# Activation buffers moved by 64 bytes within their partition, in a two-block transformer kernel in float32 precision

## The reference, cut to what matters

```
# first block, per layer
h = rms_norm(x, g) * (1 + sc1) + sh1
x = x + g1 * hybrid_mixer(h)               # w_in, two linear-attention halves, w_out
h = rms_norm(x, g) * (1 + sc2) + sh2
x = x + g2 * ((silu(h @ w1) * (h @ w3)) @ w2)       # layer 0, hidden width 2816
x = x + g2 * sum_e gate_e * swiglu(h, w1[e], w3[e], w2[e])   # layer 1, 8 experts, top 2
# second block, per layer: ffn, mixer (short convolution, then latent attention), ffn
h_x = h_x + 0.5 * m[2] * swiglu(pre(h_x)) ; h_c the same for the context
```

## Time and profile before

| | |
|---|---|
| device time, median of 3 runs | 2835.23 us (2834.12 to 2836.9) |
| the profiled execution | 2839.29 us |
| its span, first to last instruction | 2837.6 us |
| mean granted clock of TensorE | 0.989 |
| busy TensorE | 2720.8 us (96%) |
| busy VectorE, ScalarE | 1913.8 us (67%), 1182.6 us (42%) |
| matmuls | 17542, each with its LDWEIGHTS |

### The profile page before, as it was taken

How to read it: one execution, slowest core, us unless ns; L and a number is a source line. 1 busy time by engine, 2 the same in 40 slices (tenths; PEclk the granted TensorE clock), 3 DMA queues, 4 the chain that set the end, 5 groups by cost and what they waited for, 6 DMA issues and landing times.

```text
span 2837.6 us, 43022 instructions
## 1 busy us (share of the span) xinstructions
PE 2720.8 (96%) x17542; PEld 2445.7 (86%) x17542; DVE 1913.8 (67%) x2703; ACT 1182.6 (42%) x1510; POOL 118.1 (4%) x227
## 2 busy tenths in 40 slices
PE   3979999999999999899999999999999999999999
PEld 3879998899999999888888888888888888886999
DVE  5877778765777788777477445764666646675655
ACT  3436445453443477642132424422334222255543
POOL 0010000000000000000000000000000000000000
PEclk9989999999999999999999999999999999999999
DMA  7676766635676698745355223453534534311554
GB/s 296 220 244 228 263 228 213 232 135 169 235 239 209 230 347 309 259 145 187 132 184 169 83 93 103 153 170 122 166 136 137 169 122 159 120 60 46 176 186 144
DMA packets 116619, 511.97 MB, mean 180 GB/s; under 512 B 12608, under 2 KB 16064, under 8 KB 116304
## 3 DMA queue, kind: packets, MB, share of 16 engines
q1 hardware_dynamic: 81776, 381.92, 39.5%
q0 software_dynamic: 32112, 117.45, 12.5%
q10 hardware_dynamic: 2544, 9.96, 0.9%
HBM read 508.24 MB, written 1.05 MB: 179 GB/s over the span
## 4 chain that ended last, share of the span: by engine, by line
PE 78%; DVE 11%; ACT 4%; issue 3%; DMA 2%; ACTq 0%; DVEq 0%; POOLq 0%
PE PS L2099 22%; PE PS L2101 22%; PE PS L2100 22%; DVE wlo L1102 5%; ACT whi L575 2%; PE PS L2293 1%; DMA ada_first<-in_adastream 1%; PE PS L2290 1%; PE PS L2289 1%; DVE ada L1134 1%; PE PS L2194 1%; DMA ada<-in_adastream 1%; PE PS L2195 1%; PE PS L2198 1%; DVE PS L1134 1%
## 5 line engine op out<-in xcount | busy, mean ns | idle before, releaser
L575 ACT ACTIVATE whi<-raw 128x1408 fp32r<-128x1408 f32 (+2 forms) x540 | 718.1, 1342 | 778.9 <-PE PS L2101 719.3
L1102 DVE TENSOR_TENSOR wlo<-raw,whi 128x1408 fp32r<-128x1408 f32 (+2 forms) x540 | 839.8, 1577 | 217.0 <-ACT whi L575 216.1
L2099 PE MATMUL PS<-h_hi,whi 128*128 128x256 f32 (+1 forms) x2656 | 859.2, 324 | 15.5 <-DVE wlo L1102 8.4
L2100 PE MATMUL PS<-h_lo,whi 128*128 128x256 f32 (+1 forms) x2656 | 858.7, 323 | 0.0
L2101 PE MATMUL PS<-h_hi,wlo 128*128 128x256 f32 (+1 forms) x2656 | 858.6, 323 | 0.0
L2099 PEld LDWEIGHTS PS<-h_hi,whi 128*128 128x128 f32 x2656 | 499.6, 188 | 64.0 <-DVE wlo L1102 11.4
L2100 PEld LDWEIGHTS PS<-h_lo,whi 128*128 128x128 f32 x2656 | 499.6, 188 | 43.1 <-issue 0.2
L2101 PEld LDWEIGHTS PS<-h_hi,wlo 128*128 128x128 f32 x2656 | 500.1, 188 | 39.6
L2099 PE MATMUL PS<-hid_hi,whi 128*128 128x256 f32 (+1 forms) x1298 | 415.3, 320 | 4.3 <-DVE wlo L1102 4.3
L2100 PE MATMUL PS<-hid_lo,whi 128*128 128x256 f32 (+1 forms) x1298 | 414.6, 319 | 0.0
L2101 PE MATMUL PS<-hid_hi,wlo 128*128 128x256 f32 (+1 forms) x1298 | 414.4, 319 | 0.0
(11 more groups left out here) (464 smaller groups left out, 3245.8 us busy)
## 6 DMA issues: line engine op xcount, KB each, us to landing
raw<-in_wstream SPq DMA_DIRECT2D x243, 704.0 KB, 4.5
raw<-in_wstream SPq DMA_DIRECT2D x176, 768.0 KB, 5.6
ada<-in_adastream POOLq DMA_DIRECT2D x222, 512.0 KB, 4.5
raw<-in_wstream SPq DMA_DIRECT2D x121, 512.0 KB, 4.0
ada_first<-in_adastream ACTq DMA_DIRECT2D x6, 1536.0 KB, 22.9
X<-in_xT SPq DMA_DIRECT2D x1, 1024.0 KB, 13.9
X<-in_ctxT SPq DMA_DIRECT2D x1, 1024.0 KB, 5.6
cond<-in_c_rows POOLq DMA_DIRECT2D x1, 1024.0 KB, 5.7
```

The costliest lines, as they stand in the source:

```text
L575: nc.scalar.activation(whi[:, (q + dp) % SLOTS, 0:n], raw[:, (q + dp) % RAW_SLOTS, 0:n], ACT.Copy).then_inc(hi_split, 1)
L1102: nc.vector.tensor_tensor(wlo[:, (q + dp) % SLOTS, 0:n], raw[:, (q + dp) % RAW_SLOTS, 0:n], whi[:, (q + dp) % SLOTS, 0:n].bitcast(F32), AL ...
L2099: mm(o, left[0], right[0], start=start, stop=False)
L2100: mm(o, left[0], right[1], start=False, stop=False)
```

## The change

Two things. A buffer of 16 floats (64 bytes), which nothing uses, is put behind `rstd`; everything allocated after it begins 64 bytes later. And `wroute_lo` (256 bytes), which had been the last buffer of the fullest layout, is taken from there and put on the space of `amp2`, since that layout had ended exactly at the end of SBUF.

```
         amp1 = sb("amp1", [PART, 2, 2, KD])
+        with ExitStack() as s:
+            wroute_lo = sb("wroute_lo", [PART, KD, N_EXPERTS], F32R, s)
         amp2 = sb("amp2", [PART, 2, 3, KD, 2])
...
         rstd = sb("rstd", [PART, 32])
+        sb("pad", [PART, 16])
...
                 wroute_hi = sb("wroute_hi", [PART, KD, N_EXPERTS], F32R, s2)
-                wroute_lo = sb("wroute_lo", [PART, KD, N_EXPERTS], F32R, s2)
```

## The result

Four runs of the changed kernel have a median of 2865.91 us (2864.76 to 2868.33), beside 2836.07 us (2834.12 to 2840.1) of the kernel before on the same chip: a ratio of 1.0105, 95% interval 1.0091 to 1.0119. The change costs 29.8 us. The forecast of 2829.6 us had the wrong sign, and the time lies outside its range of 2808 to 2850.

The account below looks back on a forecast made before the run. TensorE, busy 96% of the span, was taken as the bound, through start-to-start matmul distance. Terms -17.5, +10.3, +1.9 and -0.3 sum to -5.6 us: 2833.7 profiled, 2829.6 against the median; range 2808 to 2850.

Parts of the forecast that it names:

- The no-effect rival: Distances between matmuls belong to their stages, not to addresses; 2835.2 us, chance 0.17.
- the zeros: Moving wroute_lo costs nothing, and DVE and ACT see no difference from the moved buffers: 0 us each.
- the line: Matmul distance read off a line through differences 0 and 192: at 128 bytes 115.4 and 231.2 ns; 2829.6 us, chance 0.38.
- Their sum stays at 346.7 to 346.8: The 256-column and 512-column distances add to the same ns at differences 0, 64 and 192.
- 256 columns, forecast -17.5 us: 8076 matmuls over h or hid, each 2.4 ns cheaper: -19.4 us, of which -17.5 kept.
- 512 columns, forecast +10.3: 4458 matmuls, each 2.3 ns dearer: +10.3 us, all of it on the path.
- streams of weights: 1584 matmuls with weights streaming 256 columns, each 2.4 ns dearer: +3.8 us, half counted, +1.9.
- the shares for what waits swallow: About a tenth of the 256-column matmuls and half of the weight-streaming effect discounted, other engines being nearly as late.
- Period of 128 bytes: h, hid and weight panels take cq's rhythm, 119.8 and 227.0 ns: +11.4 us, 2846.6 us, chance 0.17.
- 512 columns alone dearer: 512 columns rise to 233.3 ns while 256-column streams stay at 117.8: +19.6 us, 2855 us, chance 0.06.
- Like 192: Difference 128 behaves as y's 192: 256 columns -32.0 us, 512 columns +19.6, together -12.4; 2822.8 us, chance 0.15.
- the six: The weighted cases: 2829.6 (0.38), 2822.8 (0.15), 2803 (0.07), 2835.2 (0.17), 2846.6 (0.17) and 2855 us (0.06).

Follow-up runs that it names:

- TensorE by itself: A separate kernel computing none of the reference: runs of 48 matmuls at stepped moving-minus-stationary address differences, nothing else running; 625.39 us.
- place 192: Changed kernel with the pad at 128 bytes instead of 64, so h and hid lie 192 mod 256 from the weights; 2847.49 us, 1.0032.
- place 0: Changed kernel with the pad at 192 bytes instead of 64, so h and hid lie 0 mod 256 from the weights; 2847.64 us, 1.0039.
- place 0 by the weights: Changed kernel with 64 bytes ahead of whi and 192 behind rstd: weights shifted, h's own address kept mod 256; 2849.03 us, 1.0045.
- 512 at 128: Changed kernel with its pad replaced by 64 bytes ahead of the 512-column stages' buffers alone; 2857.12 us, 1.0068.
- 512 at 0: Changed kernel with its pad replaced by 192 bytes ahead of the 512-column stages' buffers, y also to difference 0; 2827.32 us, 0.9967.
- 512 at 0, 256 at 192: Against the changed kernel: 256-wide buffers 128 bytes later than before the change, 512-wide ones 192, y to difference 0; 2820.02 us, 0.9932.

## Why the prediction was wrong, by its own steps

**Right: place relative to the weights is what counts, mod 256.** The runs with both operands shifted, with the weights alone shifted and with the 256-byte pad show it, and so do the repeated places of TensorE by itself. The test set in the prediction, `y` from 233.3 to 227.0 ns, came out at 226.7 to 227.2. The no-effect rival falls. The Trainium skill says in TensorE: Matmul & The Clock Gate, "Step-by-step: what each phase is for", that with two independent SBUF ports the next tile's load takes nothing from the running matmul. What the prediction drew from that, one distance at every placement, does not hold for this operand type: with TensorE alone at work the placement of one operand against the other moved 512 columns from 226.7 to 234.1 ns. No run shows whether it is read bandwidth that is lost.

**Right: the zeros.** The move of `wroute_lo`, DVE's 424 ns, ACT, and `y`'s -0.3 us (measured -0.4).

**Wrong: the line.** The step that failed is "I take the line through 0 and 192, because the placement at 64 lies on it". It gave 115.4 and 231.2 ns at 128; the kernel has 118.91 and 232.73. Two things were wrong in it. The point for 256 columns at 192 was one of two rhythms (113.3 and 117.8, mean 115.5 in the run with `h` there), so it was no property of the place; the earlier trace rows had shown that a place can have both, and the prediction set it aside as a doubt about addresses instead of one about its own readings. And three points on a line were taken for a law: the fourth place is not on it for either length. "Their sum stays at 346.7 to 346.8" was the same accident: at 128 it is 118.9 + 232.7 = 351.6.

In the terms of the sum: 256 columns, forecast -17.5 us, measured 8607 x 1.37 ns x 0.9 = +10.6; 512 columns, forecast +10.3, measured 4454 x 3.84 = +17.1; streams of weights, forecast +1.9, measured 1483 x 4.4 / 2 = +3.3; `y` -0.4. Together +30.6, and the runs say +29.8. So the shares for what waits swallow were sound, as far as 2 us tell; the two distances were not. The counts were a little short: the earlier trace rows leave out groups, and the trace has 8892 matmuls of `h` and `hid` with 256 columns where the prediction has 8076, and 4746 with 512 where it has 4458. At the measured distances the missing 288 of 512 columns are worth 1.1 us; no sign hangs on them. The same arithmetic, with the distances of each trace, gives the others:

| kernel | 256 / 512 columns, ns | worked out, us | measured, us |
|---|---|---|---|
| place 192 | 115.52 / 233.33 | -15.6 + 19.8 + 2.5 = +6.7 | +10.3 |
| place 0 | 119.90 / 226.70 | +18.3 - 9.8 + 4.1 = +12.6 | +10.4 |
| place 0 by the weights | 119.91 / 226.70 | +18.4 - 9.8 + 4.1 = +12.7 | +12.1 |
| 512 at 128 | 117.50 / 232.99 | +18.3 + 1.2 = +19.5 | +21.9 |
| 512 at 0 | 117.65 / 226.70 | -9.8 + 2.7 = -7.1 | -7.9 |
| 512 at 0, 256 at 192 | 115.74 / 226.69 | -12.0 + 2.4 - 9.8 + 2.4 = -17.0 | -16.9 |

(The 2.7, the first 2.4 of the last row and the 1.2 are the 1167 steps with 256 columns that read the 512-wide buffers; the last term of rows 1, 2, 3 and 6 is the streams. A difference of two medians is known to some 3 us.)

**The rivals.** "Period of 128 bytes" had the right sign and the 256-column distance almost (119.8; measured 118.9), but `h` at 128 is not `h` at 0: 232.7 against 226.7 ns for 512 columns. "512 columns alone dearer" (2855) was the nearest, with the larger of the two terms right, and had 6 in 100. "Like 192" had 512 columns right and missed with 256.

**The range.** Both measured distances lie within the bounds that the prediction had written down, 113.0 to 119.8 and 227.0 to 233.3 ns. At the dear end of both, its own terms give 14.5 + 19.6 + 5.4 = +39.5 us, 2875. The range stopped at 2850 because no case let both lengths get dearer. Three of the six let one get cheaper when the other got dearer, as in the unproven sum, and the only case with a dearer length and no cheaper one, 2855, was left out of the range.

**What stays open.** Inside TensorE, that its two reads of SBUF get in each other's way at some places is an inference: it fits the dependence on their difference, on the stationary operand's width, and the absence of other traffic, but no run looks at the reads themselves, and 512 columns at place 0, which got slower with a load half as wide (226.7 to 229.8 ns), do not fit its simple form. Open too is what picks the rhythm at places 64 and 128.

## What to carry to other kernels

Where TensorE is busy in all of a stage, count matmuls per stretch and read start-to-start distances: they show a cost that has no wait and no instruction. With new weights for each matmul in this operand type, treat the moving buffer's address minus the weight panel's, mod 256 bytes, as a tuning parameter by width of the stream (here 0 for 512 columns, 192 or 64 for 256), and measure each place; never fill one in from its neighbours. When two costs are unknown, take the range over both ends of each, unless a run shows that they move together.

## What the runs showed of the hardware

- Streams of fp32r matmuls, each with its own 128-column load: 512 columns take 226.7 ns at place 0, 228.9 at 64, 232.2 to 233.4 at 128 and 192; 256 columns take 120.0 at 0, 117.8 at 64 (in the large kernel now and then 113.4), 118.4 to 120.0 at 128, and 113.3 or 117.8 at 192. The prediction's 213.3 ns for the bare streaming of 512 columns occur at no place.
- Two rhythms at one placement (113.3 and 117.8 ns at places 64 and 192) that nearly always hold for as long as the stream is not interrupted, and at place 192 are chosen by the length of the one matmul ahead.
- With 128 and with 192 moving columns a matmul takes the same 111.7 ns. The Trainium skill, TensorE: Matmul & The Clock Gate, "LDWEIGHTS (loading the stationary operand)", gives columns / 1.2 ns for a load; for 128 columns this makes an estimate of 106.7 ns, and the measured distance is 5 ns above it.
- A shift of every activation buffer by 64 bytes, which changes no instruction but its addresses, is worth 1% of this kernel.
